# Compression's products with the inputs stationary in four column groups, followed by a product that selects, in a two-block kernel on one core

## The reference, cut to what matters

```python
CMP_LEN = 32; CMP_STRIDE = 16; CMP_HIDDEN = 128   # head dimension hd = 64

def _compress(tok, pos_emb, w1, w2):
    B, S, hd = tok.shape
    n_cmp = (S - CMP_LEN) // CMP_STRIDE + 1          # 15 blocks of 32 tokens
    idx = np.arange(n_cmp)[:, None] * CMP_STRIDE + np.arange(CMP_LEN)[None, :]
    blocks = tok[:, idx] + pos_emb
    hid = jax.nn.gelu(blocks.reshape(B, n_cmp, CMP_LEN * hd) @ w1)   # 2048 -> 128
    return hid @ w2

kc = _compress(k_cmp, cmp_pos_k, cmp_w1_k, cmp_w2_k)
vc = _compress(v_cmp, cmp_pos_v, cmp_w1_v, cmp_w2_v)
g = jax.nn.sigmoid(p['g_merge'].reshape(B, S, 3, D_MODEL))     # the "gate" blocks
```

## Time and profile before

| | us |
|---|---|
| three runs, median (lowest to highest) | 751.03 (749.55 to 751.15) |
| the profiled execution | 750.67 |
| its span in the profile | 748.6 |

### The profile page before, as it was taken

How to read it: one execution, slowest core, us unless ns; L and a number is a source line. 1 busy time by engine, 2 the same in 40 slices (tenths; PEclk the granted TensorE clock), 3 DMA queues, 4 the chain that set the end, 5 groups by cost and what they waited for, 6 DMA issues and landing times.

```text
span 748.6 us, 14960 instructions
## 1 busy us (share of the span) xinstructions
PE 741.5 (99%) x6348; PEld 732.2 (98%) x6348; DVE 601.3 (80%) x897; ACT 376.7 (50%) x506; POOL 30.6 (4%) x22
## 2 busy tenths in 40 slices
PE   8999999999999999999999999999999999999998
PEld 8999999999999999999999999999999999999998
DVE  4756889899897778998998888979788886687554
ACT  6558255654666543443434666266556553434330
POOL 0000000004000000000000000301110000000000
PEclk9999999999999999999999999999999999999999
DMA  8844373332743459999887526655344565688511
GB/s 334 310 155 154 110 281 113 109 126 102 309 177 138 158 185 365 361 333 338 324 310 276 181 102 225 226 184 210 112 169 142 198 226 176 228 278 303 199 57 57
DMA packets 24113, 156.07 MB, mean 208 GB/s; under 512 B 3568, under 2 KB 3696, under 8 KB 6000
## 3 DMA queue, kind: packets, MB, share of 16 engines
q1 hardware_dynamic: 24048, 155.13, 57.7%
HBM read 154.07 MB, written 1.05 MB: 207 GB/s over the span
## 4 chain that ended last, share of the span: by engine, by line
PE 95%; DVE 2%; DMA 1%; ACT 1%; issue 1%; SPq 0%; DVEq 0%
PE bank L803 17%; PE bank L804 16%; PE bank L805 16%; PE bank L886 9%; PE bank L888 9%; PE bank L889 9%; PE bank L811 3%; PE bank L813 3%; PE bank L814 3%; PE bank L1294 2%; PE bank L1261 1%; DMA sb_raw<-in_stream 1%; PE bank L1271 1%; PE bank L1191 1%; PE bank L1335 0%
## 5 line engine op out<-in xcount | busy, mean ns | idle before, releaser
L1770 DVE TENSOR_TENSOR sb_lo<-sb_raw,sb_hi 128x2048 fp32r<-128x2048 f32 (+1 forms) x114 | 259.2, 2277 | 72.7 <-ACT sb_hi L1425 72.4
L1425 ACT CAST sb_hi<-sb_raw 128x2048 fp32r<-128x2048 f32 (+1 forms) x114 | 215.5, 1895 | 99.6 <-PE bank L889 49.6
L803 PE MATMUL bank<-sb_u_hi,sb_hi 128*128 128x256 f32 (+1 forms) x688 | 193.1, 281 | 0.0
L805 PE MATMUL bank<-sb_u_hi,sb_lo 128*128 128x256 f32 (+1 forms) x688 | 190.5, 277 | 0.0
L804 PE MATMUL bank<-sb_u_lo,sb_hi 128*128 128x256 f32 (+1 forms) x688 | 190.5, 277 | 0.0
L803 PEld LDWEIGHTS bank<-sb_u_hi,sb_hi 128*128 128x128 f32 (+1 forms) x688 | 128.9, 187 | 2.8 <-issue 2.2
L804 PEld LDWEIGHTS bank<-sb_u_lo,sb_hi 128*128 128x128 f32 (+1 forms) x688 | 129.2, 188 | 0.0
L805 PEld LDWEIGHTS bank<-sb_u_hi,sb_lo 128*128 128x128 f32 (+1 forms) x688 | 129.0, 187 | 0.0
L886 PE MATMUL bank<-sb_hid_hi,sb_hi 128*128 128x256 f32 x432 | 119.3, 276 | 0.0
L888 PE MATMUL bank<-sb_hid_lo,sb_hi 128*128 128x256 f32 x432 | 119.2, 276 | 0.0
L889 PE MATMUL bank<-sb_hid_hi,sb_lo 128*128 128x256 f32 x432 | 119.2, 276 | 0.0
(11 more groups left out here) (370 smaller groups left out, 1335.4 us busy)
## 6 DMA issues: line engine op xcount, KB each, us to landing
sb_raw<-in_stream SPq DMA_DIRECT2D x140, 1024.0 KB, 5.2
sb_raw<-in_stream SPq DMA_DIRECT2D x4, 256.0 KB, 6.4
sb_raw<-in_stream SPq DMA_DIRECT2D x2, 512.0 KB, 9.0
sb_mem_t<-in_mem SPq DMA_DIRECT2D x1, 1024.0 KB, 4.8
out<-sb_h SPq DMA_DIRECT2D x4, 256.0 KB, 2.2
sb_const<-in_constants SPq DMA_DIRECT2D x1, 830.0 KB, 11.1
sb_h<-in_x SPq DMA_DIRECT2D x1, 572.0 KB, 3.8
sb_h<-in_x SPq DMA_DIRECT2D x1, 512.0 KB, 6.7
```

Source lines behind the costliest of these rows:

```text
L803: nc.tensor.matmul(out, a_hi, b_hi, start=(i == 0), stop=False)
L805: last = nc.tensor.matmul(out, a_lo, b_hi, start=False, stop=(i == n - 1))
L1425: nc.scalar.copy(place(hi, s)[:, 0:n], x[:, 0:n]).then_inc(sem("hi_ready"), 1)
L1770: tt(place(lo, s)[:, 0:n], x[:, 0:n], f32(place(hi, s)[:, 0:n]), ALU.subtract) \
```

## The change

The 16 products of an input are made with the operands changed over: stationary are 32 columns of `cmp_in` (two neighbouring groups k, of which only one belongs to the weights used), moving are the 128 columns of piece k of `w1`. Product k writes partitions 32(k mod 4) to 32(k mod 4)+31 of a bank, so that four follow each other in four column groups of the array. All 16 stand ahead of the gate block. ACT copies the 128 x 128 partial sums into `cmp_parts`, a part of `prob_t` that is free then. Between the halves of the gate block a further fp32 product, `cmp_sum`, has the partial sums stationary and a constant 0/1 matrix `pick` of 16 columns moving: it picks the right half of each group of 32 and adds the four groups. Its result stands in the bank as before, and all that follows is the same. On ACT the tanh of gate block 2 stands behind the copy for input 0; for input 1 no such move is made. SP now waits for the partial sums before it loads over `w1`. `pick` widens the constants by 16 columns; an unused gap is narrowed by as much.

```diff
@@ constants and plan
-                    ..., cmpneg=2 * NC, cmp01=2 * NC, decay=RH * 2 * P)
+                    ..., cmpneg=2 * NC, cmp01=2 * NC, pick=16, decay=RH * 2 * P)
+    put("pick", (i % 32 - 16 * (i // 32 % 2)) == np.arange(16)[None, :])
-    block("gate", 2, between=[("pv_stick", 3), ("o_group", 0), ("turn_cmp", 1), ("index", 0), ("rope1", 3)])
-    steps([("cmp_product", 0, 0)])
-    block("gate", 3, between=[("cmp_product", 0, 1), ("cmp_hidden", 0), ("topk", 0, 0)])
-    steps([("cmp_product", 1, 0), ("topk", 0, 1), ("turn_qk", 2)])
-    block("gate", 4, between=[("cmp_product", 1, 1), ("cmp_hidden", 1), ("cmp_hid",), ("topk", 0, 2)])
+    block("gate", 2, evac_now=False, between=[("pv_stick", 3), ("o_group", 0), ("turn_cmp", 1), ("index", 0), ("rope1", 3)])
+    steps([("cmp_product", 0)])
+    evac(where["gate", 2])
+    block("gate", 3, between=[("cmp_sum", 0), ("cmp_hidden", 0), ("topk", 0, 0)])
+    steps([("cmp_product", 1), ("topk", 0, 1), ("turn_qk", 2)])
+    block("gate", 4, between=[("cmp_sum", 1), ("cmp_hidden", 1), ("cmp_hid",), ("topk", 0, 2)])
@@ tiles
-        sb(ctx, "gap", [P, P // 4])
+        sb(ctx, "gap", [P, P // 4 - 16])
+        cmp_parts = prob_t[:, 0, 0:256].rearrange("p (i n) -> p i n", i=2)
@@ TensorE
-            def cmp_product(i, part):
+            def cmp_product(i):
-                key = ("cmp_hidden", i)
+                key = ("cmp_parts", i)
                 w = shaped(raw_ready(pe, ("cmp_w1", i)), ("cmp_w1", i))
-                ps = banks[lease[key][0]] if part else claim(key, "turn")
+                ps = claim(key, "turn")
                 pe.wait_ge(sem("cmp_in_ready"), i + 1)
-                x = cmp_in[:, i, :].rearrange("p (k n) -> p k n", k=16)
-                for k in half(16, part):
-                    last = nc.tensor.matmul(ps[:, 0:16], w[:, k, :], x[:, k, :], start=(k == 0), stop=(k == 15))
-                if part:
-                    fill(last, key)
+                for k in range(16):
+                    r = slice(32 * (k % 4), 32 * (k % 4) + 32)
+                    pair = 16 * (k - k % 2)
+                    last = nc.tensor.matmul(ps[r, 0:P], cmp_in[:, i, pair:pair + 32], w[:, k, :], start=(k < 4),
+                                            stop=(k >= 12), skip_group_check=True)
+                fill(last, key)
+            def cmp_sum(i):
+                wait_evacuated(pe, ("cmp_parts", i))
+                ps = claim(("cmp_hidden", i), "turn")
+                fill(nc.tensor.matmul(ps[:, 0:16], cmp_parts[:, i, :], cst("pick"), start=True, stop=True),
+                     ("cmp_hidden", i))
@@ ScalarE
+            def cmp_product(i):
+                key = ("cmp_parts", i)
+                ps = wait_filled(act, key)
+                free(nc.scalar.copy(cmp_parts[:, i, :], ps[:, 0:P]), key)
@@ SyncE
-                        wait_filled(sp, ("cmp_hidden", before[1]))
+                        wait_filled(sp, ("cmp_parts", before[1]))
```

More of the change, by code:

```diff
@@ L61 @@
 CONST_WIDTHS = dict(ident=P, suffix=P, prefix=P, ones=P, causal=2 * P, strict=3 * P, cos1=64, sin1=64, nsin1=64,
-                    cos2=128, sin2=128, nsin2=128, cmpneg=2 * NC, cmp01=2 * NC, decay=RH * 2 * P)
+                    cos2=128, sin2=128, nsin2=128, cmpneg=2 * NC, cmp01=2 * NC, pick=16, decay=RH * 2 * P)
 CONST_AT = dict(zip(CONST_WIDTHS, np.cumsum([0] + list(CONST_WIDTHS.values())).tolist()))
@@ L177, in steps @@
             else:
-                if step[0] == "cmp_product" and step[2] == 0:
+                if step[0] == "cmp_product":
                     raw.append(("cmp_w1", step[1]))
@@ L1383, in _ @@
             run(dict(block=take, mem_v=mem_v, raw=raw_product, ssq_cols=ssq_cols, rstd_row=rstd_row, turn_qk=turn_qk, turn_tail=turn_tail, stick=stick, suffix=suffix,
-                     pv_stick=pv_stick, index=index, turn_cmp=turn_cmp, cmp_product=cmp_product, cmp_kv=cmp_kv,
+                     pv_stick=pv_stick, index=index, turn_cmp=turn_cmp, cmp_product=cmp_product, cmp_sum=cmp_sum, cmp_kv=cmp_kv,
                      cmp_scores=cmp_scores, turn_cmp_p=turn_cmp_p, cmp_pv=cmp_pv, scores=scores, turn_p=turn_p,
@@ L1682, in _ @@
                  "turn_qk": turn_qk, "turn_tail": turn_tail, "stick": stick, "suffix": suffix, "gates_c": gates_c,
-                 "cmp_hidden": cmp_hidden,
+                 "cmp_product": cmp_product, "cmp_hidden": cmp_hidden,
                  "cmp_kv": cmp_kv, "cmp_scores": cmp_scores, "turn_cmp_p": turn_cmp_p, "scores": scores,
```

## The result

| | before | after |
|---|---|---|
| median, us (lowest to highest) | 749.45 (748.26 to 751.67), 16 runs | 752.73 (751.21 to 754.69), 16 runs |
| ratio to before, 95% interval | | 1.0040 (1.0029 to 1.0051) |
| the profiled execution, us; its span | see the table ahead | 753.18; 751.4 |
| TensorE's granted clock, mean of the profiled execution | see there | 0.995 |

The account below looks back on a forecast made before the run. Up to 119.64 us it took TensorE's queue and the DVE/ACT chain as nearly equal bounds. TensorE's 4.0 us saving goes into the wait: 750.67 - 0.3 = 750.4, 750.7 on the median's scale, stated as 750.6; range 749.3 to 752.8.

Parts of the forecast that it names:

- X = 1.2 us: TensorE's cost of one input's 32 compression passes if four column groups run side by side, changeover included.
- the upper bound: 7.2 us a compression product on TensorE, if column groups do not run side by side and weight loads do not hide.
- rival A: Column groups do not run side by side in the two products: 751.9 us, or 758.7 with unhidden loads; chance 0.08.
- The wait for ACT, 3.5 us: TensorE idles 3.5 us before the second selecting product, until ACT's copy behind gate block 3's tanh is done at 100.26.
- The small wait behind `turn_qk`: TensorE may wait for DVE to take input 0's result; this would only move idle time forward.
- What the wait does to the clock, put at nothing: After idling before the second selecting product, TensorE goes on at 100.31 with no clock loss in the sum.
- rival B: TensorE's clock falls in the 3.5 us idle time; 4.4 us at half rate lose 2.2 us: 752.4 us; chance 0.10.
- The end of the step, 0.3 us earlier: After the second selecting product, TensorE's next matmul starts at 100.65 instead of 100.95; DVE also begins 0.3 us earlier.
- the other half of the argument: DVE and ACT's chain limits the gain up to 119.64: 0.3 us forecast, DVE never more than 0.49 us earlier.
- Behind it nothing is changed: Both chains reach 119.64 us 0.3 us earlier, and the rest of the kernel runs as before.

Follow-up runs that it names:

- kernel 1: The changed kernel with 14 idle products on TensorE ahead of the second selecting product's wait; 750.95 us, ratio to before 1.0015.
- experiment 5: The changed kernel with 7 idle products on TensorE ahead of the second selecting product's wait; 751.31 us, ratio to before 1.0010.
- experiment 3: The kernel before with all 16 old-form compression products of an input in one piece ahead of the gate block; 752.07 us, ratio 1.0037.
- experiment 11: The changed kernel with 14 idle products in the wait, plus a small memset on POOL ahead of its first merge addition; 750.25 us, ratio to before 0.9999.
- Kernel 9: The changed kernel with gate block 3's eviction behind the second copy and nine idle products in the waits at `scores` 4 and 5; 750.36 us, ratio 1.0001.
- kernels 2 and 6: 2: changed kernel, gate block 3's eviction behind the second copy, ratio 1.0016; 6: the same without the first tile's last two top-k parts, 1.0001.

## Why the prediction was wrong, step by step

The measured median, 752.73 us, lies within the stated range (749.3 to 752.8), but that is luck. The range was laid about the median of three runs of the kernel before, 751.03, and 16 runs gave 749.45. Its upper end allowed 1.8 us more than before, through the fallen clock, to which it gave one chance in ten; the change costs 3.0.

- **Column groups, X = 1.2 us: right,** measured 1.01 from its first pass to the next block's first matmul. So 32 passes on all 128 rows in four column groups do hide their weight loads and run side by side. The rule of the Trainium skill, page "TensorE: Matmul & The Clock Gate", section on packing small matmuls, which would have put a product near the upper bound, does not hold here; with it rival A falls. The selecting product took 0.14 us in the first place, where 0.22 was put.
- **The wait for ACT, 3.5 us: right,** 3.36. Its parts came as written: tanh to copy 0.53 us, the copy 0.25 us against 0.28. All times stand about 0.4 us earlier than the prediction's, which went by one execution; 99.07 in place of 99.45 is nearly the same offset as 84.64 in place of 85.11. The small wait behind `turn_qk`, named there (0.43 us for DVE), only moved idle time forward.
- **What the wait does to the clock, put at nothing: this step failed.** The prediction timed the wait itself rightly and then assumed that TensorE goes on behind it as it had worked before it ("TensorE goes on at 100.31 ... 0.3 us earlier"), and gave the fallen clock, its own rival B, 0.10. It happened in the profiled execution and, by the mean clocks, in all but one of the other 15. Its price was put at 2.2 us of TensorE's path for a spell of 4.4 us; the trace shows 2.7 for one of 6.8. Experiments 1 and 5 settle it: with the same wait filled, in experiment 5 by half, and nothing else changed, 1.9 and 2.2 us come back.
- **Why 0.10 was too little.** No row of before had an idle time of that length, and the prediction took the absence for a reason against the effect. But one row spoke: at the start, after standing still, passes ran at half pace; the prediction used it for the price and not for the chance. The compression products of the kernel before also stood in halves between gate matmuls. What splitting them protects shows in experiment 3: in one piece, without any wait, they lower the clock by themselves.
- **The end of the step, 0.3 us earlier: right where the clock is kept.** From the last matmul of gate block 2 to the first of the second half of gate block 4 both profiles of before take 15.96 us. Kernels 1, 5 and 11, with the wait of the prediction and the clock at 1.00, take 15.78, 15.60 and 15.77, so 0.2 to 0.4 us less. The kernel after takes 15.98, since its selecting product already runs at half rate (0.41 us from 100.00 to 100.41, where 0.22 was put). Kernel 9 shows the other half of the argument: 0.9 us ahead at 119 us, it waits for DVE and goes on 0.3 us ahead.
- **"Behind it nothing is changed": wrong by about 0.5 us.** DVE's residue at 177 us started 0.12 us ahead of POOL's second addition in the kernel before and starts 0.07 us behind it in the kernel after (0.08 in kernel 1); these 0.2 us turned round which of the two is held up (experiment 11). TensorE then stands idle for 0.6 us at the `out` blocks instead of 0.2.
- **The sum as measured:** the 0.3 us gained did not come (0.0), the clock costs 2.75, 0.4 come back at 119 to 124 us, where the kernel before waits for DVE (rival B had 0.2), and DVE and POOL cost 0.5: some 2.8 us, against 3.0 (2.2 to 3.8) by the runs. The two profiles of before alone differ by 0.2 us from the first product to the end.

What stays open: how the chip judges TensorE's activity (runs of one kernel differ, from 0.995 to 1.000 in the kernel after), what chooses between the paces of 0.113 and 0.118 us at one granted clock, and whether the memset shortens the whole kernel at all.

## What to carry to other kernels

A wait that only takes up time saved is not free on TensorE: ask in what state the engine comes out of it, and if the gap is longer than any that the trace has at full clock, price the work behind it at 1.2 GHz and compare with filling the gap with idle products. Before a product is made cheaper, look at what the next waits on that engine are; here the order of ACT and DVE left 0.2 to 0.4 us to win of 4. Behind a shift of 0.2 us look at every place where VectorE and GpSimd work at the same time.

## What the runs showed of the hardware that was not expected

- The granted clock fell without any idle time: towards the end of 32 passes with 16 columns moving, 3.6 us of them, it went from 1.00 to 0.50 (experiment 3). In kernels 2 and 6 it fell at waits of 0.8 to 1.2 us that lie between small groups.
- A wait of 1.90 us behind 7 idle products left the clock at 1.00 in the profiled execution, one of 3.36 us without them did not. In the second profile of before TensorE stands still for 1.80 us ahead of its first product at 8 us, and the clock stays at 1.00.
- Sixteen fp32 products of 128 columns moving in four column groups took 1.01 us, where the same products the other way round (16 columns moving, whole array) took 3.40.
- At one granted clock, 1.00, matmuls of 256 columns followed each other at 0.113 us in some stretches and 0.118 in others, not the same ones in two executions of one kernel (53 and 55 matmuls from 188 to 194 us). This moves a profile by 0.5 to 0.8 us in places.
- A difference of 0.17 us in which of DVE and POOL comes first (0.08 ahead, 0.09 behind) made a DVE instruction 3.36 or 2.29 us long and two POOL additions 2.54 or 4.61 us.
